# Two more columns at the end of the tokens stage, and sums loaded two joins ahead, in a hybrid decoder step

## The chip, the cores and the metric

The kernel runs on one core of a Trainium2 chip. Times are device microseconds of that core. Three runs of the kernel before took 2443.08, 2441.34 and 2442.59 us; the median is 2442.59.

## What is computed

One inference step of a one-layer hybrid trunk, for a prompt of 2048 tokens and 8 sampled sequences of 4 new tokens (32 tokens), width 1024. Cut to what matters here:

```python
u = rmsnorm(h, norm_mix_g)
proj = u @ w_in                       # q, k, v of A and C | z | xbc | dt
oa = banded_attention(A)              # window 128, with a sink per head
oc = sum over branches of w_b * o_b   # C: (128,1), (512,4), (2048,16), weighted by their denominators
xbc = silu(causal_dwconv(xbc))        # width 4, 1024 channels
dt = softplus(dt_raw + dt_bias); y = ssd_chunked(x, dt, A, B, C) + d_skip * x
ob = rms_normalize(y * silu(z)) * ssm_norm_g
h = h + [oa | ob | oc] @ w_out
h = h + square(relu(rmsnorm(h) @ w_up)) @ w_down
```

## The kernel before, in words

Every float32 product is made of three float16 matmuls (high by high, high by low, low by high). The kernel has three stages, each a block of its own with its own semaphores: `tokens`, `settle` (GpSimd clears semaphores) and `core`.

**The tokens stage** (`tokens`, L92) computes the normed input u, stores its halves, and makes the columns of q, k, v and dt by token. It also turns the weights of the 12 "z" columns (z and xbc, 128 channels each) into halves (`z_w`, two places), stores them to `kept_w`, and makes those columns for the 32 sampled tokens. `Z_ORDER` ends with 4 and 5, so at the end `z_w` holds the weights of the first two columns of the channel phase. Four more, those that were handled first, are loaded back into the ring (`load_ahead`, L328 to L332, semaphore `ahead_in`). Its last units are "ahead" 0, a "half", "silu", a "half" and "ahead" 1 (its `plan`, L162). An "ahead" (L789 to L794) is one column of the channel phase for the first 512 tokens: 24 matmuls of 128x512, whose bank is left to the next stage. SP's queue ends with the last stores and waits until all have landed.

**The core stage** (`core`, L828) first has the channel phase: 4 pieces of 512 tokens by 12 columns, each column four "quarters" of 6 matmuls. Weights of a column come through a ring of 5 places (`fetch`, L1319; `RING`, `RING_AHEAD` and `COL_AHEAD` in L820). ScalarE copies a finished column out of its bank (`take_col`, two instructions), VectorE filters it if it is one of the first 8 (`conv`, three instructions and a copy), and after every fourth column ScalarE has a "silu" with a table load before and behind it.

Beside the quarters, a hand-made plan (`plan`, L1063) hangs the other work on positions 48n + 4i + quarter. Attention begins at 4 COL_AHEAD + 1: 16 tiles of the dilation 16 at a spacing of 3 quarters, then the 12 of the first block at 3 or 4. In slot k TensorE gives values of tile k-3, turns p of tile k-2 and makes the scores of tile k-1. VectorE makes the maxima, ScalarE the exponentials and the high halves of p, VectorE the low halves. "dt" has two parts, at columns 4 and 7 of the first piece (L1090); its first needs eight small loads (`dt_in`, 128) and is work of VectorE and ScalarE alone. The sampled tokens' scan begins at position 38. Then follow the scans of chunks 0 to 3, each with parts at 0, 7 and 11 quarters, and four joins: "weigh" t on VectorE combines the stored outputs and denominators of four attention kinds (`js`, one tile of 128 x 4 x 264, loaded by `load_sums`, L1454), and "turn" t transposes the result on TensorE into u, with copies on ScalarE and subtractions on VectorE. The load of join t+1 waits for join t. A spacing of 6 quarters lies between the joins. "ahead" 0 and 1 in this stage split the first raw weights of "out". "out 0" needs all four turns and the scans' mix, loaded by `load_scanned` after turn 2.

Every engine works through its own instructions strictly in the order of the units, and so does SP, which issues all loads and stores. After the channel phase come "out", the norm, "up" and "down" of each of the four blocks; attention, scans and joins of the next block run beside them.

In the trace, L2421 is every dense matmul of the core stage, L793 those of "ahead" in tokens, L2516, L2531 and L2546 values, turned p and scores, L2752 the turns of joins. L2131 is the filter, L2064 the maxima, L1834 the exponentials, L1827 and L2083 the halves of p, L1767 and L1768 the silu with its loads.

```python
            at = 4 * COL_AHEAD + 1
...
                        if n == 0 and i in (4, 7) and quarter == 0:
                            yield "dt", i // 7, 0, 0
```

Of the kernel before, what the change touches and what calls it, by code (L numbers as in the profile page):

```python
# [91 lines left out]
def tokens(nc, io, before):  # L92

    with ExitStack() as ctx:
# [205 lines left out]
        with nc.Block() as block:  # L301
# [404 lines left out]
            def _(pe):  # L706
# [57 lines left out]
                for kind, n, j, q in units:  # L764
# [24 lines left out]
                    elif kind == "ahead":  # L789
                        free(pe, "ahead", j)  # L790
                        for k in range(KT):
                            for i, (part, s) in enumerate(((0, 0), (0, 1), (1, 0))):
                                pe.matmul(prod[ahead_bank[j]][:, :], z_w[:, j % 2, k, part, :], u[:, 0, s, k, 0:512], start=k == 0 and i == 0,  # L793
                                          stop=k == KT - 1 and i == 2)  # L794
# [25 lines left out]
RING, RING_AHEAD, COL_AHEAD = 5, 4, 2  # L820
# [7 lines left out]
def core(nc, io, before):  # L828

    with ExitStack() as ctx:  # L830
# [30 lines left out]
        R, RW, AHEAD, SP_H = RING, 2, 2, 4  # L861
        NH = KT + SP_H
# [34 lines left out]
        v_lo = a.sb("v_lo", [P, RV, 4, HD + 1], F16)  # L897
        p = a.sb("p", [P, 4, 2 * P])
# [16 lines left out]
        with ExitStack() as early:  # L915
# [60 lines left out]
        js = a.sb("js", [P, 4, OROW])  # L976
        jt = a.sb("jt", [P, 2, 256])
# [7 lines left out]
        js_in, j_step, j_exp, j_ready, j_turned, jh_ready, jl_ready, j_out = (  # L985
            a.sem(s) for s in ("js_in", "j_step", "j_exp", "j_ready", "j_turned", "jh_ready", "jl_ready", "j_out"))
# [76 lines left out]
        def plan():  # L1063
# [17 lines left out]
            for unit in joins(0):  # L1081
                beside[at].append(unit)
                at += 6 if unit[0] == "weigh" else 0
# [197 lines left out]

        def raw_src(q):
# [8 lines left out]
        def loads(q):  # L1291

            return sum(1 for j in range(q % R, q + 1, R) if not raw(j) and j >= RING_AHEAD)
# [22 lines left out]
        with nc.Block() as block:  # L1316
            @block.sync
            def _(sp):
                def fetch(q):  # L1319
# [11 lines left out]
                    else:  # L1331
                        sp.dma_start(ring[:, q % R, :, :, :].rearrange("p k i c -> p (k i c)"), kept_w[home(q), :, :]).then_inc(ring_in[q % R], 16)

                def keep(q):
                    if raw(q):
                        sp.wait_ge(lo_split, raw_no[q] + 1)
                        sp.dma_start(kept_w[home(q), :, :], ring[:, q % R, :, :, :].rearrange("p k i c -> p (k i c)")).then_inc(kept[q % R], 16)
# [116 lines left out]
                def load_sums(t):  # L1454
# [70 lines left out]
                def finish(unit):  # L1525
# [29 lines left out]
                    elif kind == "weigh" and b % 4 < 3:  # L1555
                        load_sums(b + 1)
# [28 lines left out]
                fetch(RING_AHEAD)  # L1585
# [15 lines left out]
                fetched, next_qkv = RING_AHEAD + 1, 3  # L1601
# [1300 lines left out]
```

## Time and profile before

| what | value |
|---|---|
| time of the runs | 2442.59 us median (2441.34 to 2443.08) |
| profiled execution | span 2443.3 us; the page gives no other time for it, and it lies 0.7 us above the median |
| TensorE busy | 2363.2 us (97%), 17246 matmuls |
| VectorE, ScalarE, GpSimd busy | 1216.1 (50%), 817.0 (33%), 272.7 us (11%) |
| DMA | 419.64 MB, mean 172 GB/s |
| granted clock, mean | 0.989 |

### The profile page before, as it was taken

To read this page: it belongs to the slowest core of one execution; us is meant where nothing else is said; L and a number is where in the kernel's file an instruction comes from. 1 tells how busy PE (TensorE), PEld (TensorE's weight loads), DVE (VectorE), ACT (ScalarE), POOL (GpSimd) and SP (SyncE) were. 2 spreads that over 40 slices of the span, in tenths; PEclk is the share of its full clock that TensorE was granted. 3 is DMA by queue.
4 is the path that set the end of the run, shared out by engine and by line. 5 is a ranking of instruction groups with operands and counts; after the bars stand their busy time and mean duration, and the time that the engine had idled before them with its cause. 6 is when DMAs were issued, how large, how long until landed. Compare 5 with 4: busy or idle time off the path is not lost. (4 is left out here: it accounts for less than half of the span.)

```text
span 2443.3 us, 42522 instructions
## 1 busy us (share of the span) xinstructions
PE 2363.2 (97%) x17246; PEld 1374.2 (56%) x17246; DVE 1216.1 (50%) x2785; ACT 817.0 (33%) x1467; POOL 272.7 (11%) x301
## 2 busy tenths in 40 slices
PE   9899889999889999999999999999999999999999
PEld 5456445555435555444555554445555456888887
DVE  5557465656647667742655563145566522322222
ACT  5544244554445444331423222023323111210210
POOL 0111223111011211001120100001111001000000
PEclk9999999999999999999999999999999999999999
DMA  7646496785477876885575565534645553222222
GB/s 254 240 162 229 167 233 168 209 234 172 146 236 180 222 213 214 268 266 164 135 171 154 163 184 159 174 119 129 166 157 170 177 160 122 88 96 96 96 96 85
DMA packets 396561, 419.64 MB, mean 172 GB/s; under 512 B 130319, under 2 KB 325391, under 8 KB 396112
## 3 DMA queue, kind: packets, MB, share of 16 engines
q1 hardware_dynamic: 396368, 416.94, 56.8%
q8 instruction: 137, 2.24, 0.4%
q14 instruction: 56, 0.46, 0.1%
HBM read 280.01 MB, written 118.96 MB: 163 GB/s over the span
## 5 line engine op out<-in xcount | busy, mean ns | idle before, releaser
L2421 PE MATMUL core_dense<-core_u,tok_ring 128*128 128x512 f16 (+2 forms) x4800 | 862.3, 340 | 7.8 <-DVE core_u L2004 7.5
L2421 PEld LDWEIGHTS core_dense<-core_u,tok_ring 128*128 128x128 f16 x4800 | 465.7, 98 | 375.6 <-DVE core_u L2004 11.4
L2421 PE MATMUL core_dense<-core_r_hi,tok_ring 128*128 128x512 f16 (+2 forms) x2560 | 649.9, 339 | 1.2 <-DVE core_r_lo L2023 1.2
L2421 PE MATMUL core_dense<-core_r_lo,tok_ring 128*128 128x512 f16 (+2 forms) x1280 | 434.1, 339 | 0.0
L2421 PEld LDWEIGHTS core_dense<-core_r_hi,tok_ring 128*128 128x128 f16 x2560 | 250.4, 98 | 195.8 <-DVE core_r_lo L2023 1.9
L2421 PE MATMUL core_dense<-tok_u,tok_ring 128*128 128x512 f16 x1104 | 259.9, 393 | 15.1 <-PEq L811 11.0
L2020 DVE TENSOR_TENSOR core_r<-core_r 128x512 f32<-128x512 f32 (+2 forms) x160 | 96.7, 605 | 293.7 <-ACT core_r L1804 293.3
L1804 ACT ACTIVATE core_r<-core_dense 128x512 f32<-128x512 f32 (+2 forms) x160 | 82.4, 515 | 478.9 <-PE core_dense L2421 478.7
L732 PE MATMUL tok_prod<-tok_w_hi,tok_u 128*128 128x512 f16 (+1 forms) x768 | 197.2, 346 | 4.1 <-DVE tok_u L601 4.1
L2421 PEld LDWEIGHTS core_dense<-tok_u,tok_ring 128*128 128x128 f16 x1104 | 107.9, 101 | 147.5 <-issue 27.6
L2421 PEld LDWEIGHTS core_dense<-core_r_lo,tok_ring 128*128 128x128 f16 x1280 | 125.2, 98 | 93.3 <-issue 0.7
L2032 DVE SCALAR_TENSOR_TENSOR core_h<-core_dense,core_h 128x512 f32<-128x512 f32 (+1 forms) x96 | 58.3, 607 | 210.4 <-PE core_dense L2421 210.3
L1834 ACT ACTIVATE core_p<-core_p,core_neg 128x256 f32<-128x256 f32 (+1 forms) x256 | 99.7, 460 | 183.3 <-DVE core_neg L2071 183.3
L732 PE MATMUL tok_prod<-tok_w_lo,tok_u 128*128 128x512 f16 (+1 forms) x384 | 132.9, 346 | 0.0
L1984 DVE SCALAR_TENSOR_TENSOR tok_ring<-core_staged,tok_ring 128x1024 f16<-128x1024 f32 x72 | 89.2, 1239 | 70.9 <-ACT tok_ring L1737 69.4
L1678 POOL TENSOR_TENSOR core_v_hi<-core_v_raw,core_ones 128x256 f16<-128x256 f32 (+1 forms) x82 | 61.2, 747 | 489.9 <-DMA core_v_raw<-out_tok 337.1
L732 PEld LDWEIGHTS tok_prod<-tok_w_hi,tok_u 128*128 128x128 f16 x768 | 73.4, 98 | 69.1 <-DVE tok_u L601 6.7
L2131 DVE SCALAR_TENSOR_TENSOR core_col<-core_conv_raw,core_cw,core_col 128x512 f32<-128x512 f32 x96 | 76.9, 801 | 63.5 <-ACT core_conv_raw L1758 61.2
L2023 DVE TENSOR_TENSOR core_r_lo<-core_r,core_r_hi 128x512 f16<-128x512 f32 (+2 forms) x160 | 96.3, 602 | 17.0 <-DVE core_r L2020 0.5
L2032 DVE SCALAR_TENSOR_TENSOR core_h_more<-core_dense,core_h_more 128x512 f32<-128x512 f32 (+1 forms) x64 | 36.2, 565 | 130.2 <-PE core_dense L2421 130.2
L1714 POOL TENSOR_TENSOR core_ssum<-core_ssum,core_r 128x512 f32<-128x512 f32 (+1 forms) x24 | 30.8, 1284 | 573.2 <-ACT core_r L1783 573.2
L2064 DVE CUSTOM_DVE_ANT_0 core_p<-core_spare,core_bias 128x256 f32<-128x256 f32 (+1 forms) x256 | 81.5, 374 | 23.4 <-PE core_spare L2546 18.0
(317 smaller groups left out, 2590.3 us busy)
## 6 DMA issues: line engine op xcount, KB each, us to landing
tok_ring<-scratch_kept_w SPq DMA_DIRECT2D x262, 512.0 KB, 4.5
scratch_kept_w<-tok_ring SPq DMA_DIRECT2D x72, 512.0 KB, 5.5
core_staged<-in_w_up SPq DMA_DIRECT2D x32, 512.0 KB, 4.8
core_staged<-in_w_down SPq DMA_DIRECT2D x32, 512.0 KB, 4.5
out_tok<-tok_tok SPq DMA_DIRECT2D x16, 644.0 KB, 3.0
core_piece<-in_c_kt SPq DMA_DIRECT2D x32, 288.0 KB, 4.0
core_piece<-in_c_v SPq DMA_DIRECT2D x16, 576.0 KB, 4.6
scratch_sums<-core_o SPq DMA_DIRECT2D x64, 132.0 KB, 3.7
```

The costliest lines, as they stand in the source:

```text
L732: last = pe.matmul(bank[0:nt, 0:w], l, r[:, k, c0:c0 + w], start=k == 0 and i == 0, stop=k == KT - 1 and i == 2, skip_group_check=True)
L1678: pool.tensor_tensor(hi, v, ones[:, 0:w].rearrange("p (h d) -> p h d", d=HD), ALU.mult).then_inc(vh_ready, 1)
L1714: pool.tensor_tensor(ssum[:, 0:w], ssum[:, 0:w], r[:, i % 2, 0:w], ALU.add).then_inc(summed, 1)
L1804: act.activation(r[:, n % 2, 0:w], bank_of["up", b, f, q][:, 0:w], ACT.Relu, scale=1.0 / (WS * HS)).then_inc(r_ready, 1)
L1834: last = act.activation(p[:, hh, cols], p[:, hh, cols], ACT.Exp, bias=neg[:, hh:hh + 1])
L1984: dve.scalar_tensor_tensor(ring[:, q % R, :, 1, :], w_raw[n % RW], WS, ring[:, q % R, :, 0, :], ALU.mult, ALU.subtract).then_inc(lo_split, 1)
L2020: dve.tensor_tensor(r2[:, n % 2, 0:w], r[:, n % 2, 0:w], r[:, n % 2, 0:w], ALU.mult).then_inc(r2_ready, 1)
L2023: dve.tensor_tensor(r_lo[:, f % HF, off:off + w], r2[:, n % 2, 0:w], r_hi[:, f % HF, off:off + w], ALU.subtract).then_inc(rl_ready, 1)
L2032: dve.scalar_tensor_tensor(here, bank_of["down", b, i, q][:, 0:w], HS * HS / WS, here, ALU.mult, ALU.add).then_inc(down_added, 1)
L2064: last = dve.tensor_tensor_reduce(p[:, hh, cols], spare[1 + bank][:, :].rearrange("p (a c) -> p a c", c=2 * P)[:, at, cols], bias[:, BIAS_ ...
L2131: dve.scalar_tensor_tensor(dst, conv_raw[:, i, j:j + 512], cw[:, i, j:j + 1], dst, ALU.mult, ALU.add).then_inc(tap, 1)
L2421: ins = pe.matmul(bank, w[:, k, part, :], s, start=first and j == 0, stop=last and j == 2, skip_group_check=True)
```

## The change

The tokens stage makes four columns ahead instead of two: the first two from `z_w`, the third and fourth from ring places 0 and 1, after a wait for the ring's loads. The core stage's first slot of the ring is then at place 2 (`place_of`), two of its columns are already loaded instead of four, and three loads are issued at the start instead of one. All that hangs on `COL_AHEAD` moves by 8 quarters; the spacing of the first block's joins is 5 quarters instead of 6. A second tile for sums, `js_odd`, lies where p and the beginning of `p_hi` are. The sums of joins b and b+1 are loaded at the second part of a block's first scan, those of join t+2 after "weigh" t.

```diff
 kind == "ahead":
                         free(pe, "ahead", j)
+                        if j >= COL_KEPT:
+                            pe.wait_ge(ahead_in, 16 * RING_AHEAD)
+                        w_ahead = z_w[:, j % 2, :, :, :] if j < COL_KEPT else ring[:, j - COL_KEPT, :, :, :]
...
-RING, RING_AHEAD, COL_AHEAD = 5, 4, 2
+RING, RING_AHEAD, COL_AHEAD, COL_KEPT = 5, 4, 4, 2
...
+        USED = COL_AHEAD - COL_KEPT
+        LOADED = RING_AHEAD - USED
...
+        with ExitStack() as early:
+            js_odd = early.enter_context(nc.sbuf_tensor("core_js_odd", [P, 4, OROW], F32))
         p = a.sb("p", [P, 4, 2 * P])
...
             for unit in joins(0):
                 beside[at].append(unit)
-                at += 6 if unit[0] == "weigh" else 0
+                at += 5 if unit[0] == "weigh" else 0
...
+        def place_of(q):
+            return (q + USED) % R
...
-                    if t:
-                        sp.wait_ge(j_ready, t)
-                    else:
+                    if t >= 2:
+                        sp.wait_ge(j_ready, t - 1)
+                    elif t == 0:
                         sp.wait_ge(ss_out, SS_ALL)
-                    sp.dma_start(js[:, :, :], io["sums"][:, t * P:(t + 1) * P, :].rearrange("k p c -> p k c")).then_inc(js_in, 16)
+                    sp.dma_start(js_of[t % 2][:, :, :], io["sums"][:, t * P:(t + 1) * P, :].rearrange("k p c -> p k c")).then_inc(js_in[t % 2], 16)
...
-                    elif kind == "weigh" and b % 4 < 3:
-                        load_sums(b + 1)
+                    elif kind == "weigh" and b % 4 < 2:
+                        load_sums(b + 2)
...
-                fetch(RING_AHEAD)
+                for q in range(LOADED, R):
+                    fetch(q)
...
-                fetched, next_qkv = RING_AHEAD + 1, 3
+                fetched, next_qkv = R, 3
...
-                    elif kind == "scan" and i == 2 and b % 4 == 3:
-                        load_sums(b - 3)
+                    elif kind == "scan" and i == 1 and b % 4 == 0:
+                        load_sums(b)
+                        load_sums(b + 1)
```

## Rows read from the trace of the kernel before

**Rows 1.** Windows by stage: length, busy us of each engine, clock, DMA share, GB/s.
```profile
309.00:345.00 36.00, 31.71 (x215) 15.03 (x215) 23.38 (x76) 20.64 (x43) 9.22 (x17) 0.91 0.95 228
632.00:684.00 52.00, 42.97 (x184) 19.37 (x183) 31.71 (x98) 20.12 (x32) 0.00 (x0) 0.89 0.58 178
```

**Rows 2.** Timeline of TensorE, 292 to 325 us: start, us, line, operation.
```profile
292.59 5.34 PE L793 MATMUL tok_prod<-tok_u,tok_z_w 128*128 128x512 f16 x24
308.92 8.30 PE L2421 MATMUL core_dense<-tok_u,tok_ring 128*128 128x512 f16 x30 [10.99 <-PEq L811]
...
324.42 0.63 PE L2531 MATMUL core_spare<-core_ident,core_p 128*128 128x128 f32 x4 [2.78 <-ACT core_p L1834]
```

**Rows 3.** The chain of waits in order of time, one column: start, us, what.
```profile
1299.34 5.18 PE core_dense L2421 x24
```

**Rows 4.** Timeline of SP's queue, 305 to 323 us.
```profile
305.20 0.55 SPq L426 DMA_DIRECT2D scratch_xc<-tok_col_s  x1
...
322.66 0.42 SPq L1594 DMA_DIRECT2D core_of_seq<-in_of_seq  x1
```

**Rows 5.** DMA issues of 290 to 345 us: count, KB, us to landing.
```profile
scratch_xc<-tok_col_s SPq DMA_DIRECT2D x1, 128.0 KB, 2.5
...
core_of_seq<-in_of_seq SPq DMA_DIRECT2D x1, 1.0 KB, 1.5
```

**Rows 6.** Timeline of VectorE, 313 to 333 us.
```profile
313.05 2.67 DVE L2131 SCALAR_TENSOR_TENSOR core_col<-core_conv_raw,core_cw,core_col 128x512 f32<-128x512 f32 x3 [11.41 <-ACT core_conv_raw L1758]
...
319.23 2.32 DVE L2131 SCALAR_TENSOR_TENSOR core_col<-core_conv_raw,core_cw,core_col 128x512 f32<-128x512 f32 x3
...
329.56 0.29 DVE L2098 TENSOR_TENSOR core_dt_all<-core_dt_all,core_dt_bias 128x136 f32<-128x136 f32 x1
...
332.94 0.21 DVE L2109 TENSOR_TENSOR core_a_seq<-core_of_seq,core_small 32x64 f32<-32x64 f32 x1
```

**Rows 7.** Timeline of ScalarE, 322 to 342 us.
```profile
322.89 1.28 ACT L1834 ACTIVATE core_p<-core_p,core_neg 128x128 f32<-128x128 f32 x4 [5.66 <-DVE core_neg L2071]
...
337.36 1.28 ACT L1767 ACT_TABLE_LOAD   x1
...
340.58 1.28 ACT L1768 ACT_TABLE_LOAD   x1
```

**Rows 8.** Windows of 2 us, columns as in rows 1.
```profile
310.00:312.00 2.00, 2.00 (x6) 0.73 (x5) 0.00 (x0) 0.82 (x2) 0.24 (x1) 0.50 0.35 71
```

**Rows 9.** Timeline of TensorE, 343 to 351 us.
```profile
343.15 0.19 PE L2516 MATMUL core_spare<-core_v_hi,core_p_hi 128*128 128x65 f16 x1 [1.44 <-issue]
...
350.23 0.19 PE L2516 MATMUL core_spare<-core_v_hi,core_p_hi 128*128 128x65 f16 x1 [1.40 <-DVE core_p_lo L2083]
```

**Rows 10.** Timeline of TensorE, 621 to 685 us.
```profile
621.89 5.35 PE L2421 MATMUL core_dense<-tok_u,tok_ring 128*128 128x512 f16 x24
...
677.27 7.03 PE L2421 MATMUL core_dense<-tok_u,tok_ring 128*128 128x512 f16 x24
684.13 41.60 PE L2421 MATMUL core_dense<-core_u,tok_ring 128*128 128x512 f16 x192
```

**Rows 11.** Waits of VectorE, 640 to 700 us: total, times, longest.
```profile
DVE core_j_m L2243 <- DMA core_js<-scratch_sums: 5.8, 3, 3.5
```

**Rows 12.** Waits of TensorE, 640 to 700 us.
```profile
PE core_spare L2752 <- DVE core_jt L2262: 9.0, 3, 5.1
```

**Rows 13.** Window of L2421 alone: busy of TensorE and its weight loads, clock, DMA, GB/s.
```profile
631.70:684.30 52.60, 41.34 (x169) 17.71 (x170) 0.89 0.57 176
```

**Rows 14.** Timeline of VectorE, 640 to 679 us.
```profile
640.70 0.16 DVE L2243 TENSOR_TENSOR core_j_m<-core_js 128x4 f32<-128x4 f32 x1 [1.67 <-DMA core_js<-scratch_sums]
...
678.16 0.76 DVE L2364 TENSOR_TENSOR core_u<-core_spare,core_u 128x256 f16<-128x256 f32 x2 [0.30 <-ACT core_u L1936]
```

**Rows 15.** DMA issues of 664 to 684 us, columns as in rows 5.
```profile
core_u<-scratch_mix_lo SPq DMA_DIRECT2D x1, 512.0 KB, 7.9
```

More of the change, by code:

```diff
@@ L790, in _ @@
                         free(pe, "ahead", j)
+                        if j >= COL_KEPT:
+                            pe.wait_ge(ahead_in, 16 * RING_AHEAD)
+                        w_ahead = z_w[:, j % 2, :, :, :] if j < COL_KEPT else ring[:, j - COL_KEPT, :, :, :]
                         for k in range(KT):
                             for i, (part, s) in enumerate(((0, 0), (0, 1), (1, 0))):
-                                pe.matmul(prod[ahead_bank[j]][:, :], z_w[:, j % 2, k, part, :], u[:, 0, s, k, 0:512], start=k == 0 and i == 0,
+                                pe.matmul(prod[ahead_bank[j]][:, :], w_ahead[:, k, part, :], u[:, 0, s, k, 0:512], start=k == 0 and i == 0,
                                           stop=k == KT - 1 and i == 2)
@@ L976, in core @@
         js = a.sb("js", [P, 4, OROW])
+        js_of = (js, js_odd)
         jt = a.sb("jt", [P, 2, 256])
@@ L984, in core @@
         j_lo = a.sb("j_lo", [P, 4, P], F16)
-        js_in, j_step, j_exp, j_ready, j_turned, jh_ready, jl_ready, j_out = (
-            a.sem(s) for s in ("js_in", "j_step", "j_exp", "j_ready", "j_turned", "jh_ready", "jl_ready", "j_out"))
+        js_in, j_step, j_exp, j_ready, j_turned, jh_ready, jl_ready, j_out = a.sems("js_in", 2), *(
+            a.sem(s) for s in ("j_step", "j_exp", "j_ready", "j_turned", "jh_ready", "jl_ready", "j_out"))
         J_STEPS = 12
@@ L1291, in loads @@
         def loads(q):
-            return sum(1 for j in range(q % R, q + 1, R) if not raw(j) and j >= RING_AHEAD)
+            return sum(1 for j in range(q % R, q + 1, R) if not raw(j) and j >= LOADED)
         def stores(q):
@@ L1331, in fetch @@
                     else:
-                        sp.dma_start(ring[:, q % R, :, :, :].rearrange("p k i c -> p (k i c)"), kept_w[home(q), :, :]).then_inc(ring_in[q % R], 16)
+                        sp.dma_start(ring[:, place_of(q), :, :, :].rearrange("p k i c -> p (k i c)"), kept_w[home(q), :, :]).then_inc(ring_in[q % R], 16)
                 def keep(q):
@@ L1336, in keep @@
                         sp.wait_ge(lo_split, raw_no[q] + 1)
-                        sp.dma_start(kept_w[home(q), :, :], ring[:, q % R, :, :, :].rearrange("p k i c -> p (k i c)")).then_inc(kept[q % R], 16)
+                        sp.dma_start(kept_w[home(q), :, :], ring[:, place_of(q), :, :, :].rearrange("p k i c -> p (k i c)")).then_inc(kept[q % R], 16)
                 def load_pu(n):
@@ L1736, in split @@
                         act.wait_ge(raw_in[n % RW], 16 * (n // RW + 1))
-                        act.activation(ring[:, q % R, :, 0, :], w_raw[n % RW], ACT.Copy, scale=WS).then_inc(hi_split, 1)
+                        act.activation(ring[:, place_of(q), :, 0, :], w_raw[n % RW], ACT.Copy, scale=WS).then_inc(hi_split, 1)
                 def take_col(n, i):
@@ L1983, in split @@
                         dve.wait_ge(hi_split, n + 1)
-                        dve.scalar_tensor_tensor(ring[:, q % R, :, 1, :], w_raw[n % RW], WS, ring[:, q % R, :, 0, :],
+                        dve.scalar_tensor_tensor(ring[:, place_of(q), :, 1, :], w_raw[n % RW], WS, ring[:, place_of(q), :, 0, :],
                                                  ALU.mult, ALU.subtract).then_inc(lo_split, 1)
@@ L2237, in then @@
                         dve.wait_ge(j_step, J_STEPS * t + count[0])
-                    dve.wait_ge(js_in, 16 * (t + 1))
+                    dve.wait_ge(js_in[t % 2], 16 * (t // 2 + 1))
+                    js = js_of[t % 2]
                     if t:
@@ L2413, in weights @@
                         pe.wait_ge(lo_split, raw_no[q] + 1)
-                    elif q >= RING_AHEAD:
+                    elif q >= LOADED:
                         pe.wait_ge(ring_in[q % R], 16 * loads(q))
-                    return ring[:, q % R, :, :, :]
+                    return ring[:, place_of(q), :, :, :]
                 def thrice(bank, w, k, hi, lo, first, last):
```

## The prediction

> **What bounds it now.** I read the windows by stage first. TensorE is the engine to watch: of the 36 us from 309 to 345 it is busy 31.7, of the 52 us from 632 to 684, where the first block is joined, 43.0 at a mean clock of 0.89 [rows 1]. The change takes no matmul away, so it can gain only TensorE's idle and half-clock time, and it touches two places where there is some: the gap between the stages, and these joins. TensorE's timeline shows the gap [rows 2]. Its list of waits names the joins' turns between 640 and 700 us, and none in later blocks. From "out 0" on only the joins' loads move.
>
> **The gap between the stages.** TensorE's last "ahead" column starts at 292.59 and takes 5.34; the next matmul comes at 308.92, after 10.99 us of idle time [rows 2]. A column of 24 matmuls takes 5.18 us at full clock [rows 3], so two more take 10.4 and end at 308.3. Today the stage's end is set elsewhere: the store of the sampled columns is issued at 305.20 [rows 4] and lands 2.5 us later [rows 5], at 307.7; core starts 1.2 us behind it. If part of that follows TensorE's end instead, core starts between 308.9 (not moved) and 309.5 (all of the 1.2); I take 309.3, 0.4 later. The new wait on "ahead_in" stands in TensorE's queue before column 2. The loads it waits for are issued with "z" 6 to 9, long before, and cost nothing; were they late, the gap would stay empty by as much.
>
> **The start of core pays it back.** Today VectorE filters columns 0 to 2, from 313.05 on, the third from 319.23 to 321.6 [rows 6]; the first scores' maxima follow, then ScalarE's exponentials at 322.89 [rows 7], and TensorE turns p at 324.42 after 2.78 us idle [rows 2]. The change shifts all attention by 8 quarter columns with the columns, but "dt 0" and the first "silu", tied to column 4, stay. So before the first p VectorE now has four filters, dt 0, the filter of column 4 and the maxima. Each start 0.4 later than today: filters from 313.4, two at 3.1 us, two at 2.45, to 324.6. Then dt 0 waits for all eight of its loads. Today the last is issued at 322.66 [rows 4] and lands 1.5 us later [rows 5], 324.2. Two more ring loads of 512 KB stand ahead of it in SP's queue: half a microsecond each to issue (the small one takes 0.42), and they share the engines, at 0.95 here [rows 1]. For that I take 0.9 us, so 326.5; below, nothing (the filters end at 324.6), above, 3 us more. dt 0 takes 3.6 us (329.56 to 333.15 [rows 6]), to 330.1; the filter 2.45, the maxima 1.2, to 333.8. ScalarE too stands behind dt 0: it takes column 4 until 329.4 and then has "silu" with its two table loads, 4.5 us as from 337.36 to 341.86 [rows 7], until 333.9; exponentials 1.3 us. TensorE turns p at **335.2** instead of 324.42: 10.8 later, the 0.4 included, having stood there since about 321, a wait of 14 us for today's 2.78. It then has 8 quarters, 10.4 us, less to do. Gap and start together: **+0.4**, between -1.5 (no load late) and +3.4. The gap is filled, and one of the same size opens behind it.
>
> The Trainium skill ("DMA: Bandwidth & Descriptors", "Queues, rings and completion order") has each DMA engine take its descriptors in ring order, which would put dt's small loads behind the big ones. At that page's 436 GB/s they would be held 2.4 us, an estimate, and p would come 1.5 us later than mine: it speaks against the change.
>
> **Half clock.** From 310 to 312, after the gap, the granted clock is still 0.50, 1.2 GHz [rows 8], and the first 30 matmuls take 8.30 us [rows 2] where 6.5 would do at 2.4. Filling the gap wins these 1.8 us, but they end in the wait for p, and behind that wait a low stretch like this one comes back. Net 0.
>
> **What hides in the new wait.** Today the silu of 337 to 342 us holds up the halves of p: TensorE is idle 1.44 us before 343.15, and 1.40 before 350.23 [rows 9]. dt 0 and this silu are over before 335.2. I take **-2.0** (0 to -2.8).
>
> **Edits that cost nothing.** Columns 2 and 3 lie in spare banks 2 and 1, where the first scores go: TensorE waits there until ScalarE has copied column 3, some 1.1 us, in front of the wait for p, which covers it. "place_of" changes addresses only; columns' weights come 42 times either way (46 slots less 4, 44 less 2). Attention and scans keep their distances to each other and to the filters; each silu meets another part of them, which I leave at 0, within 2 either way. In later blocks load_sums stands at the first chunk's second part, two columns of work after the last attention unit, with SP in step with TensorE, so its stores have landed and nothing queues behind it; js_odd shares p's place, idle by then.
>
> **The joins.** In all they take 56.9 us today, from the end of quarter 163 (621.89 + 5.35 = 627.24) to "out 0" at 684.13 [rows 10]; 46.5 without the 8 quarters that move away. In them, VectorE waits 5.8 us for js in three of four joins [rows 11], TensorE 9.0 for VectorE [rows 12], and its dense matmuls from 631.7 on take 41.3 us for seven columns [rows 13], 5 more than 7 x 5.2. Afterwards VectorE never waits for js, but a join has 5 quarters (6.5 us) instead of 6, and its own 4.8 us (from 640.70 [rows 14] to 645.5) stay. Counting from T, the end of quarter 171: scan 3's sums on TensorE to T+4.7 as today, norm and halves on VectorE to T+8.1, join 0 to T+12.9; TensorE waits 2 us, then turns. Filter, subtraction and join 1 end at T+20.9, 0.8 late. silu 3,1 on ScalarE delays turn 1's copies, so join 2 ends at T+30.1, 2.0 late; join 3 at T+37, in time. Turn 3 now stands behind the last column, not 4 quarters before it. Its copies and subtractions, 1.6 us (677.27 [rows 10] to 678.92 [rows 14]), are uncovered: "out 0" at T+39.4. A load is late next. The scans' mix is loaded after turn 2, and SP's queue now has the raw load for "out 2" ahead of it, which waits for VectorE's split behind join 2. So issue at T+31.9 and two loads; today the second landed 7.9 us after issue [rows 15], 7 to 10 us for the pair: T+40.7 in the middle. Half clock adds 1.0: 41.7 instead of 46.5, **-4.8**; at best -11.6 (no turn waits, full clock), at worst -1 (the quarter less per join eats what the loads give).
>
> **Sum.** +0.4 - 2.0 - 4.8 = -6.4 us on the profiled span of 2443.3, 2436.9. The span is 0.7 above the runs' median of 2442.59; on the median's scale **2436.2 us**.
>
> **Rivals.** (a) The gap is filled and nothing is paid back: -10.4, joins -9.0, half clock -4.5, 2418.7. Against it: VectorE and ScalarE have no way round dt 0. 7%. (The Trainium skill, "TensorE: Matmul & The Clock Gate", "Why this matters for your kernels", has idle gaps between bursts closed to keep the clock up; by that rule alone the change gains.) (b) As forecast, but no turn waits: joins -11.6, 2429. For it: later blocks. 18%. (c) Within 0.2%: joins -1, start 1 worse, silu's gain 1: 2442. For it: VectorE's chain of filter, subtraction and join is longer than 5 quarters. 25%. (d) Slower: dt's loads land far behind the ring loads. It decides from 338 for them, p turned at 346.5; up to there the joins pay. With p at 347.5 it is 2448.5. Against it: they land 1.5 us after issue today [rows 5]. 8%. My own forecast: 42%.
>
> Two tenths of a per cent (4.9 us) is about what a measurement of this kernel can tell from no change. Below 2437.7 lie (a), (b) and most of my own case: 0.60. Within it 0.32, slower 0.08. The range reaches from just beyond (b) to just beyond (c), 2427 to 2443, and leaves out (a), (d) and the bounds' far ends.
>
> **What would show it.** Right: "ahead" without a gap to 308.3; core from 308.9 to 309.5; one wait of TensorE of 12 to 16 us before the first turn of p, with dt 0 ahead of column 4's filter; no wait of VectorE for js; turns' waits of 4 to 5 us in all; 1 to 3 us before "out 0". Wrong: p turned before 331 (then (a)); a gap left before "ahead" 2; new waits over 3 us between 345 and 632; any difference behind "out 0".

## The result and the profile after

| | before | after |
|---|---|---|
| median of the runs, us | 2442.14 (2441.34 to 2443.08) | 2458.53 (2458.08 to 2460.32) |
| ratio, 95% interval | | 1.0065 [1.0053, 1.0077] |
| profiled span, us | 2443.3 | 2456.6 |
| TensorE busy, us | 2363.2 | 2366.6 |

The change makes the kernel slower by 0.65%, 16.4 us on the medians and 13.3 us between the two profiled executions. The forecast was 2436.2 us, with a range of 2427 to 2443: wrong, and on the other side.

The 3.1 us between the two differences lie in the profile of before. In 135 executions of these kernels the time is 1.7 to 3.0 us above the span, 1.9 in the middle; so a span of 2443.3 belongs to an execution of about 2445, an estimate, some 3 us above the median. Two runs with the plan of before (e2 and e11, below) have 217.3 and 217.6 us in the stage from P0 to X0 where this profile has 219.2.

The line numbers of the core stage are 15 higher in the kernel after (14 for VectorE and ScalarE): L2421 is now L2436, turned p L2546, values L2531, the sums of a scan L2682 (before L2667), the joins' turns L2767.

The timeline of TensorE after, 292 to 338 us, answers to [rows 2]:
```profile
292.16 5.34 PE L796 MATMUL tok_prod<-tok_u,tok_z_w 128*128 128x512 f16 x24
297.34 10.52 PE L796 MATMUL tok_prod<-tok_u,tok_ring 128*128 128x512 f16 x48
308.86 6.63 PE L2436 MATMUL core_dense<-tok_u,tok_ring 128*128 128x512 f16 x30 [1.00 <-PEq L814]
316.38 0.51 PE L2561 MATMUL core_spare<-core_qk_t 64*128 64x128 f16 x12 [0.89 <-ACT core_conv_raw L1772]
...
336.07 1.09 PE L2546 MATMUL core_spare<-core_ident,core_p 128*128 128x128 f32 x4 [15.19 <-ACT core_p L1848]
```
The gap is filled, as meant: two more columns in 10.52 us, 1.00 us of idle time, the core stage's first matmul still at 308.9, and its first 30 in 6.63 us for 8.30. And a wait of 15.19 us stands before the first turn of p. So far all is as forecast.

To see where the time went I cut both traces at six events that lie at the same place of the work: the core stage's first matmul, the first turn of p (P0), the 17th turn (P16), the first matmul of chunk 0's scan (X0), the sums of chunk 3's scan (G3) and "out 0". These are the windows of after, with the columns of [rows 1]:
```profile
308.90:336.10 27.20, 11.12 (x61) 4.90 (x61) 16.93 (x38) 14.05 (x22) 6.05 (x14) 0.80 0.85 212
336.10:476.50 140.40, 129.99 (x1019) 71.67 (x1020) 77.84 (x292) 61.63 (x142) 34.96 (x45) 0.91 0.73 199
476.50:563.70 87.20, 83.34 (x769) 46.58 (x768) 51.93 (x183) 50.33 (x95) 10.12 (x16) 1.00 0.73 201
563.70:660.70 97.00, 79.62 (x474) 43.42 (x472) 56.41 (x119) 40.26 (x53) 15.73 (x12) 0.94 0.55 170
660.70:696.70 36.00, 32.27 (x144) 15.56 (x145) 27.50 (x91) 16.75 (x29) 0.00 (x0) 0.92 0.52 157
```
and the same windows of before:
```profile
308.90:324.40 15.50, 12.73 (x60) 5.26 (x61) 9.46 (x21) 6.49 (x12) 6.22 (x14) 0.89 0.81 160
324.40:457.10 132.70, 124.25 (x1019) 69.02 (x1020) 81.01 (x300) 66.29 (x148) 34.55 (x43) 0.95 0.80 216
457.10:543.60 86.50, 83.02 (x770) 46.54 (x769) 52.37 (x183) 50.09 (x96) 11.39 (x18) 1.00 0.77 208
543.60:629.90 86.30, 78.28 (x473) 42.73 (x471) 56.24 (x119) 35.77 (x50) 15.61 (x12) 0.98 0.57 179
629.90:684.10 54.20, 45.16 (x192) 21.34 (x193) 32.63 (x99) 22.20 (x34) 0.00 (x0) 0.88 0.56 172
```
The counts of matmuls show that the cuts are fair: the middle three windows hold the same work, and the last 48 matmuls less, the 8 quarters (10.4 us) that went ahead. Start +11.7, P0 to X0 +8.4, scans +10.7, joins -18.2, all behind "out 0" +0.7: +13.3 us. The joins without the quarters gained 7.8 us. Most of the loss is between P0 and G3. There the change adds nothing but the early loads of the sums; for the rest it shifts attention, scans and joins against what is tied to a column.

The list of waits of TensorE from 563 to 661 us, where the scans are, says on whom (before: 4.1 us in 2, longest 2.7, for the first kind, 2.7 for the second, none of the third):
```profile
PE core_dense L2436 <- ACT core_col L1772: 6.7, 1, 6.7
PE core_spare L2682 <- ACT core_m L1902: 4.8, 1, 4.8
PE core_dense L2436 <- ACT core_conv_raw L1772: 4.6, 1, 4.6
```
All three are for ScalarE, and a silu lengthens each, by three different ways. ScalarE's timeline ahead of the wait for core_conv_raw, which ended at 625.42:
```profile
609.75 1.28 ACT L1781 ACT_TABLE_LOAD   x1
611.04 1.91 ACT L1781 ACTIVATE core_col<-core_col 128x2048 f32<-128x2048 f32 x1
612.97 1.28 ACT L1782 ACT_TABLE_LOAD   x1
614.26 0.38 ACT L1892 ACTIVATE core_b_tok<-core_spare 128x256 f32<-128x256 f32 x1
614.54 1.05 ACT L1894 ACTIVATE core_grown<-core_dec 128x1024 f32<-128x1024 f32 x1
619.45 1.06 ACT L1896 ACTIVATE core_dec<-core_dec 128x1024 f32<-128x1024 f32 x1 [3.85 <-DVE core_dec L2214]
```
A silu of 4.5 us now stands in front of the first work of a scan (b by token), so the scan's later products come late, and the copy of a column, queued behind them on ScalarE, with them. Before, the silu at 599.43 lay behind a scan's products and held up nothing there: ScalarE's next instruction, at 604.38, waited 0.44 us more, for GpSimd.

The next silu, 649.25 to 653.75, holds back the copy of a column, and with it VectorE, whose filter stands in front of the scan's y; y then passes GpSimd and ScalarE before TensorE's sums at 660.68. VectorE's timeline of after:
```profile
655.06 2.33 DVE L2145 SCALAR_TENSOR_TENSOR core_col<-core_conv_raw,core_cw,core_col 128x512 f32<-128x512 f32 x3 [3.27 <-ACT core_conv_raw L1772]
```
The longest wait, 6.72 us before 598.65, goes through SP's queue. The silu of 574.25 ends its work at 577.46; SP waits for it with the store of its result, and the loads of the sums and of chunk 1's rows of decays stand behind that store:
```profile
577.49 0.36 SPq L1361 DMA_DIRECT2D scratch_xc<-core_col  x1
...
578.57 0.89 SPq L1474 DMA_DIRECT2D core_js<-scratch_sums  x1
...
580.80 0.66 SPq L1457 DMA_DIRECT2D core_dec<-scratch_decay  x1
```
and ScalarE has to wait for the rows:
```profile
588.42 1.06 ACT L1894 ACTIVATE core_grown<-core_dec 128x1024 f32<-128x1024 f32 x1 [3.89 <-DMA core_dec<-scratch_decay]
```
The rows' load is issued 17.1 us behind X0; before it was 13.5 (557.13), ahead of the silu's store at 577.73.

### The profile page after: what moved, and what is told of

It reads as the page before. It is cut to its first block and busy times, and to the rows that moved or that the text cites. A ratio compares the mean times of both kernels' runs of the same rounds, so it can differ in the third digit from the quotient of the medians.

```text
span 2456.6 us, 42525 instructions
## 1 busy us (share of the span) xinstructions
PE 2366.6 (96%) x17246; PEld 1376.5 (56%) x17246; DVE 1215.7 (49%) x2785; ACT 817.3 (33%) x1467; POOL 272.7 (11%) x301
## 5 line engine op out<-in xcount | busy, mean ns | idle before, releaser
L2436 PE MATMUL core_dense<-core_u,tok_ring 128*128 128x512 f16 (+2 forms) x4800 | 862.3, 340 | 9.6 <-DVE core_u L2018 7.5
L2436 PEld LDWEIGHTS core_dense<-core_u,tok_ring 128*128 128x128 f16 x4800 | 465.6, 98 | 377.4 <-DVE core_u L2018 11.4
L2436 PE MATMUL core_dense<-core_r_hi,tok_ring 128*128 128x512 f16 (+2 forms) x2560 | 650.0, 339 | 1.2 <-DVE core_r_lo L2037 1.2
L2436 PE MATMUL core_dense<-core_r_lo,tok_ring 128*128 128x512 f16 (+2 forms) x1280 | 434.1, 339 | 0.0
L2436 PEld LDWEIGHTS core_dense<-core_r_hi,tok_ring 128*128 128x128 f16 x2560 | 250.4, 98 | 195.8 <-DVE core_r_lo L2037 1.9
L2436 PE MATMUL core_dense<-tok_u,tok_ring 128*128 128x512 f16 x1056 | 250.1, 395 | 12.4 <-ACT core_col L1772 6.7
L2436 PEld LDWEIGHTS core_dense<-tok_u,tok_ring 128*128 128x128 f16 x1056 | 104.1, 101 | 141.9 <-issue 20.9
L2436 PEld LDWEIGHTS core_dense<-core_r_lo,tok_ring 128*128 128x128 f16 x1280 | 125.2, 98 | 93.3 <-issue 0.7
L2046 DVE SCALAR_TENSOR_TENSOR core_h_more<-core_dense,core_h_more 128x512 f32<-128x512 f32 (+1 forms) x64 | 36.1, 565 | 130.2 <-PE core_dense L2436 130.2
L2078 DVE CUSTOM_DVE_ANT_0 core_p<-core_spare,core_bias 128x256 f32<-128x256 f32 (+1 forms) x256 | 81.4, 373 | 25.6 <-PE core_spare L2561 19.6
```

The costliest lines, as they stand in the source:

```text
L2046: dve.scalar_tensor_tensor(here, bank_of["down", b, i, q][:, 0:w], HS * HS / WS, here, ALU.mult, ALU.add).then_inc(down_added, 1)
L2078: last = dve.tensor_tensor_reduce(p[:, hh, cols], spare[1 + bank][:, :].rearrange("p (a c) -> p a c", c=2 * P)[:, at, cols], bias[:, BIAS_ ...
L2436: ins = pe.matmul(bank, w[:, k, part, :], s, start=first and j == 0, stop=last and j == 2, skip_group_check=True)
```

## The experiments

My theory: units that the plan ties to a column (the silus, "dt", the sampled tokens' scan at 38 + 3k) stayed while attention and scans moved by 8 quarters, and where they now meet, an engine that works in order holds up TensorE. Rivals: the early loads of the sums stand in SP's queue in front of a scan's rows; four columns ahead cost something of their own. The unchanged kernel ran beside each group. Stages are from one profile each; "start" is to P0.

| run | start | P0 to X0 | scans | joins | ratio to before, 95% interval |
|---|---|---|---|---|---|
| before | 15.5 | 219.2 | 86.3 | 54.2 | |
| after | 27.2 | 227.6 | 97.0 | 36.0 | 1.0065 [1.0053, 1.0077] |
| e1_only_ahead | 27.4 | 227.3 | 96.2 | 41.4 | 1.0091 [1.0076, 1.0106] |
| e2_only_sums | 15.5 | 217.3 | 86.1 | 46.9 | 0.9982 [0.9973, 0.9991] |
| e3_scan_moved_too | 27.6 | 223.1 | 98.1 | 36.0 | 1.0060 [1.0045, 1.0075] |
| e4_sums_behind_rows | 26.1 | 232.5 | 96.2 | 36.1 | 1.0078 [1.0061, 1.0094] |
| e5_plan_only | 25.6 | 225.8 | 94.3 | 41.2 | 1.0069 [1.0054, 1.0084] |
| e7_whole_plan | 20.9 | 219.5 | 87.3 | 41.8 | 1.0011 [1.0001, 1.0020] |
| e8_silus_only | 26.3 | 227.7 | 87.3 | 40.3 | 1.0040 [1.0026, 1.0054] |
| e9_dt_only | 20.9 | 227.4 | 97.0 | 36.0 | 1.0039 [1.0024, 1.0054] |
| e10_plan_and_joins | 21.2 | 222.3 | 85.5 | 38.9 | 0.9994 [0.9985, 1.0002] |
| e11_only_sums_again | 15.8 | 217.6 | 86.0 | 47.8 | 0.9985 [0.9976, 0.9994] |
| e12_filters_behind_scores | 13.0 | 227.2 | 87.2 | 38.9 | 0.9983 [0.9974, 0.9991] |

Joins are compared after adding 10.4 us wherever four columns were made ahead or attention was moved (all but before, e2 and e11).

**The two halves of the change.** e1 is after, with the joins' loads of before:
```diff
-                    elif kind == "weigh" and b % 4 < 2:
-                        load_sums(b + 2)
+                    elif kind == "weigh" and b % 4 < 3:
+                        load_sums(b + 1)
...
-                    elif kind == "scan" and i == 1 and b % 4 == 0:
-                        load_sums(b)
-                        load_sums(b + 1)
+                    elif kind == "scan" and i == 2 and b % 4 == 3:
+                        load_sums(b - 3)
```

> The changed kernel with the joins' part undone: one tile of sums, each load one join ahead, issued after the third scan part as before. Four columns are still made ahead and the joins' spacing stays 5. Theory A (work that moved meets work that stayed): TensorE's stretch from the first turn of p to the first one of block 0 stays near 140.4 us (132.7 before). Theory B (the sums' loads stand ahead of chunk 1's rows in SP's queue): the stretch from the first scan to the last scan's sums falls from 97.0 by about 4 us, and ScalarE no longer waits 3.9 us for those rows. The joins lose again: from the last scan's sums to out 0 about 36 + 8 = 44 us. By both the whole is 3 to 6 us slower than the changed kernel.

e2 is after, with the columns and the plan of before:
```diff
-RING, RING_AHEAD, COL_AHEAD, COL_KEPT = 5, 4, 4, 2
+RING, RING_AHEAD, COL_AHEAD, COL_KEPT = 5, 4, 2, 2
...
-at += 5 if unit[0] == "weigh" else 0
+at += 6 if unit[0] == "weigh" else 0
```

> The changed kernel with two columns made ahead, as before, and the joins' spacing back at 6; two tiles of sums and their loads two joins ahead stay. Theory A: everything up to the first scan is as in the kernel before. Theory B: the stretch from the first scan to the last scan's sums is 2 to 4 us over 86.3, through a late load of chunk 1's rows. The joins gain: from 54.2 us to about 43 (no wait of VectorE for sums, no wait of TensorE for a turn). By B the whole is 6 to 9 us faster than the kernel before, without B's cost 11 us.

Measured: e1 2465.65 us, e2 2437.98, before 2442.24. The whole loss comes with the columns (start, P0 to X0 and scans of e1 are those of after), and the sums alone gain: joins 46.9 for 54.2, scans untouched at 86.1. The rival about SP's queue falls for the most part: the loads cost the scans of e2 nothing. Both expectations missed in size: e1 is 7.1 us slower than after where I had 3 to 6, and e2 gains 4.3 us where I had at least 6, since its joins came to 46.9 and not 43; TensorE still waits 4.4 us for two of the turns.

**Sums behind the rows.** The early loads moved behind the rows' load of the next chunk:
```diff
                     elif kind == "scan" and i == 1 and b + 1 < NT:
                         load_rows(b + 1)
+                        if b % 4 == 0:
+                            load_sums(b)
+                            load_sums(b + 1)
```

> The changed kernel with the two loads of sums issued behind the load of chunk 1's rows, not ahead of it. Theory B: ScalarE's wait of 3.9 us for core_dec goes, TensorE's wait of 6.7 us for a bank after it falls to 3 or less, the whole is 3 to 4 us faster. Rival (the silus' new places in the scans make this wait): the rows come early, the wait stays over 5 us, and the time changes by less than 1.5 us.

Measured: ScalarE's wait for the rows falls from 3.9 to 0.9 us and TensorE's behind it from 6.7 to 3.8, nearly as theory B had it. But the scans as a whole only go from 97.0 to 96.2, with 1.6 us less between chunks 1 and 2 (27.6 to 26.0) and 0.8 more behind them. So the order in SP's queue costs about 1 us here. The run as a whole is 4.7 us slower than after, from the stage P0 to X0 (232.5 for 227.6), which comes before the edit, and where TensorE's waits behind P0 are nearly the same (10.9 us in all up to P16, 10.1 in after); its clock is at 0.69 from 372 to 376 and 0.50 from 376 to 380, where after has 1.00. It isn't the profiled execution alone: the four runs took 2460.12 to 2464.76 us, those of after 2458.08 to 2460.32. Why the clock is lower in them isn't shown.

**The sampled scan moved with attention.**
```diff
-beside[38 + 3 * k].append(("sscan", k, 0, 0))
+beside[46 + 3 * k].append(("sscan", k, 0, 0))
```

> The changed kernel with the sampled tokens' scan moved by 8 quarters too (46 + 3k instead of 38 + 3k), so that it stands to attention as before. Theory A: the stretch from the first turn of p to the first one of block 0 falls from 140.4 us to 133 to 135, TensorE's waits for core_o in the sampled scan's sums go from 3.4 us to 0.5, and the whole is 5 to 7 us faster than the changed kernel. Rival (these losses come from the longer start alone, whose delayed work is caught up only later): no change within 2 us.

Measured: 4.5 us less between P0 and X0 (223.1). P0 to P16 takes 135.4 us for 140.4, with TensorE's busy time back at 124.0 us and its clock at 0.95, as before (124.3, 0.95); the 2.7 us that are left to before's 132.7 are idle time. Scans 1.1 more, the whole 2457.62 us, 0.9 less than after where I had expected 5 to 7. Part of the cost, not most of it.

**The plan alone.** The kernel before, with two columns ahead as ever, but attention and what follows 8 quarters later and 5 quarters between joins:
```diff
-            at = 4 * COL_AHEAD + 1
+            at = 4 * COL_AHEAD + 9
-                at += 6 if unit[0] == "weigh" else 0
+                at += 5 if unit[0] == "weigh" else 0
```

> The kernel before with nothing but its plan shifted: attention, scans and joins 8 quarters later in the channel phase (first position 17 instead of 9) and joins 5 quarters apart. Two columns are made ahead, sums have one tile. TensorE has the same columns to do, so the shift by itself costs nothing but its last part; what it costs beyond is the price of meeting silu, dt and the sampled scan, which stay. Theory A (moved work meets work that stayed): from the first turn of p to the first of block 0 it takes 5 us more than the 132.7 of before, from the first scan to the last scan's sums 95 to 97 us instead of 86.3; the whole is 12 to 20 us slower than the kernel before. Rival (the losses come from the four columns made ahead: filters and copies piled up at the start): these stretches stay within 2 us of before, and the whole within 5 us.

Measured: 2460.48 us, slower by 0.69%. This run settles it: there is no third and fourth column ahead, no other ring and no second tile in it, and it shows after's late start (here the 8 quarters themselves fill it), its middle stage within 1.8 us, and in the scans three waits of the same kinds, two of them of the same length:
```profile
PE core_spare L2667 <- ACT core_m L1888: 4.8, 1, 4.8
PE core_dense L2421 <- ACT core_conv_raw L1758: 4.6, 1, 4.6
PE core_dense L2421 <- ACT core_col L1758: 3.8, 1, 3.8
```
Beside e1 (same plan, gap filled) it also shows what the filled gap is worth: P0 comes at 334.8 us here and at 335.9 there. Two columns moved into the gap only lengthen the wait behind it.

**Silus alone, dt alone, and the whole plan.** e8 puts each silu two columns later, e9 the dt units (to columns 6 and 8), e7 both (dt at 6 and 9) and the sampled scan.
```diff
-if quarter == 3 and i % 4 == 0 and (n or i):
+if quarter == 3 and i % 4 == 2 and (n or i > 2):
...
-if n == 0 and i in (4, 7) and quarter == 0:
+if n == 0 and i in (6, 8) and quarter == 0:
```

> The changed kernel with only the silus moved by two columns. Theory A puts the loss in the scans on the silus' new places: from the first scan to the last scan's sums 86 to 89 us instead of 97.0; the first turn of p comes 4 us sooner, since silu 0 no longer stands before the exponentials; the whole 10 to 14 us faster. Rival (sums ahead of the rows, or low clock): the scans' stretch stays over 94 us, the whole within 5 us.

> The changed kernel with dt's two parts at columns 6 and 8 instead of 4 and 7. If dt and the wait for its loads are what lies in the start's chain, the first turn of p comes 21 to 23 us after the start of core instead of 27.2; if the four filters alone set it, over 25. The rest as in the changed kernel (the whole 3 to 6 us faster) unless dt's later place meets attention.

> The changed kernel with all the rest of the plan moved by 8 quarters as well: the sampled scan at 46 + 3k, dt at columns 6 and 9, each silu behind the third column of the next four instead of the first. So all work stands to all other as before, and to the columns. Theory A: first turn of p 21 us after the start of core (27.2 in the changed kernel, 15.5 before: two more filters stay ahead of it), then 133, 87, 86 to 87 and, for the joins, 36 to 38 us; the whole 20 to 25 us faster than the changed kernel, 5 to 12 faster than the kernel before. Rival (pile-up of filters at the start, sums ahead of the rows): the scans' stretch stays over 92 us and the whole is over the kernel before.

Measured: e8 brings the scans from 97.0 to 87.3, e9 the start from 27.2 to 20.9; the other's stage stays nearly where it was (start 26.3 in e8, scans 97.0 in e9). In e8 the rows' load is issued 13.5 us behind X0 again, with the sums' loads still ahead of it, and ScalarE doesn't wait for it. TensorE's timeline in e8 has the three waits of the scans at before's size (2.7, 1.4 and 2.7) or near it:
```profile
594.18 4.16 PE L2436 MATMUL core_dense<-tok_u,tok_ring 128*128 128x512 f16 x12 [2.72 <-ACT core_col L1772]
618.59 2.10 PE L2436 MATMUL core_dense<-tok_u,tok_ring 128*128 128x512 f16 x6 [2.10 <-ACT core_conv_raw L1772]
650.46 1.16 PE L2682 MATMUL core_spare<-core_m,core_ones 128*128 128x128 f32 x8 [1.44 <-ACT core_m L1902]
```
Both kernels as a whole are 4.5 us faster than after. For e9 that is what I expected, for e8 I had 10 to 14: its start came 0.9 us sooner and not 4, since ScalarE then waited for VectorE's maxima until 333.93, its joins are 4.3 us longer, and so is, by 5.2 us, all behind "out 0".

With all three moved (e7) the middle stage is back too, at 219.5 (2 us above e2 and e11), and the kernel at 2445.91 us: of 0.65% lost, 0.11% is left. I had expected 5 to 12 us less than before, so in the whole the rival is right. Its joins are 5.8 us longer than after's, because the last piece's silus now fall among them: on ScalarE the one of 670.33 stands in front of turn 3's copies, which end at 676.93. TensorE's timeline of e7:
```profile
650.12 1.12 PE L2767 MATMUL core_spare<-core_ident,core_jt 128*128 128x128 f32 x4 [6.22 <-DVE core_jt L2277]
...
678.03 22.34 PE L2436 MATMUL core_dense<-core_u,tok_ring 128*128 128x512 f16 x91 [3.70 <-issue]
```
The stretch behind "out 0" took 5.0 us more in e7's profile than before, and 5.9 in e8's. Of that, 2.5 us in e7 and 1.7 in e8 directly follow the wait of 3.70 us that both have there: the first 24 matmuls of "out 0" took 7.7 and 6.9 us for 5.2 before, at a clock of 0.74 and 0.83 in the first 10 us for 1.00. The rest stays open.

**The silus out of the joins' way.** e10 is e7 with the last piece's first silu behind "weigh" 0 and its second at quarter 179, its place in after; e11 repeats e2 beside it. The edit doesn't quite do what the expectation says of it: on ScalarE the first silu (646.42) stands in front of turn 0's copies and the second (658.22) in front of turn 1's, not behind the joins' copies.
```diff
-                        if quarter == 3 and i % 4 == 2 and (n or i > 2):
+                        if quarter == 3 and i % 4 == 2 and (n or i > 2) and not (n == 3 and i > 2):
...
+                        if (n, i, quarter) == (3, 8, 3):
+                            yield "silu", 3, 1, 0
...
                         yield from beside.pop(48 * n + 4 * i + quarter, [])
+                        if (n, i, quarter) == (3, 6, 3):
+                            yield "silu", 3, 0, 0
```

> The changed kernel with every unit that stood at a fixed place of the plan (the sampled scan, the two dt units, the silus) moved with the rest, as in the whole-plan run, but with the last piece's silus put behind scan 3's weighing and behind the joins' copies. My theory (what was lost is all in units that stayed behind while attention and scans moved, the joins' gain is real and independent): first turn of p 20.9 us after the core stage's start, from there to the sampled scan's first matmul 219 to 220, scans about 87, last scan's sums to out 0 36 to 38, span near 2433 and 0.3 to 0.5% faster than before. Rival (two columns more in front of the core stage cost something of their own that no placement gives back): scans or the stage before them stay 5 us or more above these, and the whole is no faster than before.

> The kernel before with only the joins' part of the change, a second time, on the same chip as the two beside it, since its first interval against before was a fifth of a per cent wide about a gain of the same size. My theory: 2434 to 2438 us, faster by 0.2 to 0.35%, last scan's sums to out 0 near 47 where before has 54. Rival (its gain was the spread of runs): within 0.1% of before though the stage is as short.

Measured: e10 2440.79, e11 2438.72, before 2442.84. e10's start, scans (85.5) and joins (38.9) came near what was expected; the whole did not: a span of 2439.5 us where near 2433 was expected. Its turns wait longer than after's, 6.0 us for 2.0:
```profile
PE core_spare L2771 <- DVE core_jt L2281: 6.0, 3, 3.2
```
and its core stage began 1.6 us later than after's. The middle stage took 222.3 us where e7, with the same plan there, took 219.5: the spread between executions, as far as the two profiles tell. e2 and e11, 21 runs of one kernel in two groups, both lie below before, by 0.18% and 0.15%. The rival of e10 is not refuted: with everything moved in step, the two columns in the gap gain nothing over e11, which has neither them nor the shift. e10's median is 2.1 us above e11's, and their intervals overlap.

**VectorE's filters behind the scores.** The wait of 8.9 us that is left before P0 in e10 is VectorE's: four columns' filters stand in front of the first maxima. e12 is e10 with those of columns 2 and up done behind attention units:
```diff
+elif kind == "col" and k == 3 and i < KT and b == 0 and i >= 2:
+    waiting.append(i)
...
 elif kind == "att":
     attention(b, i, k)
+    for _ in range(2 if b == 0 and k else 0):
+        if waiting:
+            conv(0, waiting.pop(0))
```

> The run with the whole plan and the joins, and in addition VectorE's filters of the first piece's columns 2 and up done behind the attention units, up to two in each, all by column 8. My theory (what TensorE waits for at the core stage's start is VectorE's chain, in which the filters of columns made ahead stand in front of the maxima): first turn of p 13.5 to 15 us after the stage's start in place of 20.9, some waits of 1 to 2 us behind it, the whole 4 to 6 us faster than the run without it, near 2428. Rival (the filters come due in the next attention units, whose VectorE work is as tight): the first turn comes earlier but the stage up to the sampled scan is longer by as much, and the whole is the same.

Measured: 2438.41 us, 2.4 us faster than e10 where I had 4 to 6. P0 comes 13.0 us after the start, 8.2 earlier, but X0 only 3.3 earlier (240.2 us from the start for 243.5; e7 has 240.4). TensorE's timeline in e12 has the rest of it:
```profile
321.78 0.63 PE L2559 MATMUL core_spare<-core_ident,core_p 128*128 128x128 f32 x4 [0.90 <-ACT core_p L1852]
...
338.13 0.21 PE L2544 MATMUL core_spare<-core_v_hi,core_p_hi 128*128 128x65 f16 x1 [4.88 <-DVE core_p_lo L2101]
```
The wait went from the maxima to the low halves of p, one engine, one chain. Mostly the rival's case. The intervals of e12 and e10 overlap, though 8 of e12's 11 runs lie below the fastest of e10's.

## Why the prediction was wrong

**The gap: right.** "Ahead" without a gap to 307.9, the wait on "ahead_in" nowhere to be seen, the core stage at 308.9 as before. The +0.4 that I had taken is there, though: the store of the sampled columns was issued at 304.74, 0.46 us sooner than in before's profile, and the core stage began no sooner.

**The start of core: right.** Forecast: P0 at 335.2 behind a wait of 14 us; measured 336.07 and 15.19. VectorE's timeline after answers to [rows 6]:
```profile
321.72 2.32 DVE L2145 SCALAR_TENSOR_TENSOR core_col<-core_conv_raw,core_cw,core_col 128x512 f32<-128x512 f32 x3
...
326.90 0.30 DVE L2112 TENSOR_TENSOR core_dt_all<-core_dt_all,core_dt_bias 128x136 f32<-128x136 f32 x1 [2.66 <-DMA core_of_seq<-in_of_seq]
...
330.29 0.21 DVE L2123 TENSOR_TENSOR core_a_seq<-core_of_seq,core_small 32x64 f32<-32x64 f32 x1
330.54 2.33 DVE L2145 SCALAR_TENSOR_TENSOR core_col<-core_conv_raw,core_cw,core_col 128x512 f32<-128x512 f32 x3
...
333.99 0.17 DVE L2085 TENSOR_SCALAR core_neg<-core_o 128x4 f32<-128x4 f32 x1
```
Filters, dt 0, column 4's filter, maxima, in this order; dt 0 began at 326.90 for a forecast of 326.5. SP's queue shows why it was late:
```profile
314.66 1.73 SPq L1344 DMA_DIRECT2D tok_ring<-scratch_kept_w  x3
...
325.30 0.42 SPq L1607 DMA_DIRECT2D core_of_seq<-in_of_seq  x1
```
The last of dt's loads was issued at 325.30 instead of 322.66 and landed 1.6 us later, for 1.5 before [rows 5]: the time was lost in issuing, not behind the ring's data. I had 1.0 us for issuing two ring loads more, and SP took 1.2 (1.73 us for three, 0.50 for one before); the other 1.5 us are in the transposing load right behind them, 2.95 us to issue for 1.45, which I didn't foresee; why it took longer isn't shown. It took the place of the 0.9 us that I had for shared engines. The estimate from the Trainium skill's rule ("DMA: Bandwidth & Descriptors", "Queues, rings and completion order"), 1.5 us more for descriptors that stand behind the ring loads, is not seen here. Gap and start cost 11.7 - 10.4 = +1.3, forecast +0.4.

**"What hides in the new wait", -2.0: not seen in the sum.** The silu of the first piece is over before P0, and its two waits [rows 9] are gone. Up to P16 TensorE's waits before values are 1.6 us shorter in all, 6.1 for 7.7. But those before the sampled scan's own matmuls are 3.5 longer, 4.0 for 0.5, and TensorE's idle time is 10.4 us for 8.5.

**"Edits that cost nothing": the step that failed.** I wrote that attention and scans keep their distances to each other, that each silu meets another part of them, "which I leave at 0, within 2 either way", and did not weigh the sampled scan's fixed place at all. Both terms are large. The silus cost the scans about 9.7 us (97.0 to 87.3 in e8), as their 4.5 us on ScalarE now stand in front of a scan's first product and before its sums instead of behind them, and the store of one in front of the rows' load in SP's queue. Between P0 and X0 the cost is 8.4 us: 4.5 come back with the sampled scan (e3), all but 0.3 with the three kinds of unit together (e7; 3.1 in e10, with the same plan there). Neither the silus alone (e8, 227.7) nor dt alone (e9, 227.4) give any of it back, so how the rest divides stays open. In the profile most of it is no wait: of the 7.7 us between P0 and P16, 5.7 are busy time for the same 1019 matmuls, at a mean clock of 0.91 for 0.95, and they are gone with the sampled scan moved (e3, 124.0). But e5, with the sampled scan in its old place, has 125.6 us too, so its place alone doesn't decide it. Together +19.1 us where I had 0; with this term the forecast of 2436.9 for the profiled span would have been 2456.0, and 2456.6 was measured, with the misses of the other steps (start +0.9, the new wait +2.0, the joins from G3 on -3.0, +0.7 behind "out 0") nearly cancelling, which is luck. The trace of before had what the step needed: the positions of the silus in the plan, and ScalarE's timeline of one scan, on which I should have moved the silu by 8 quarters, as I did for dt 0 at the start.

**"Half clock", net 0.** At the gap 1.7 us were won (30 matmuls in 6.63 us for 8.30). Behind the new wait a low stretch came back: four turns of p took 1.09 us for 0.63, the 18 dense matmuls behind them 6.21 for 5.75. The further low stretches in the attention stage, above, were not foreseen.

**The joins: right.** From G3 on they gained 7.8 us (36.0 for 54.2 - 10.4). But I had counted from T, the end of quarter 171, with the scan's sums as today: that is 655.86 here, and "out 0" came 40.9 us later for a forecast of 41.7, so -5.6 for -4.8. The other 2.2 us are the longer wait before those sums (4.82 for 2.67), which my -4.8 didn't hold and which is on the scans' account here. VectorE waits for no js any more. TensorE's timeline, all its waits between G3 and "out 0":
```profile
660.68 2.08 PE L2682 MATMUL core_spare<-core_m,core_ones 128*128 128x128 f32 x8 [4.82 <-ACT core_m L1902]
671.50 0.66 PE L2767 MATMUL core_spare<-core_ident,core_jt 128*128 128x128 f32 x4 [0.36 <-DVE core_jt L2277]
679.28 0.66 PE L2767 MATMUL core_spare<-core_ident,core_jt 128*128 128x128 f32 x4 [0.64 <-DVE core_jt L2277]
687.40 0.66 PE L2767 MATMUL core_spare<-core_ident,core_jt 128*128 128x128 f32 x4 [1.00 <-DVE core_jt L2277]
696.72 3.61 PE L2436 MATMUL core_dense<-core_u,tok_ring 128*128 128x512 f16 x16 [1.74 <-issue]
```
The turns wait 2.0 us where I had 4 to 5: TensorE waited 1.00 us for join 2, which I had 2.0 late behind silu 3,1, and 0.36 for join 0, for which I had 2. Before "out 0" there are 1.74, in the 1 to 3 foreseen.

**The rivals.** None is what happened. (d) came out on the right side for another reason, dt's loads, which were 0.4 us late; (a) is refuted by P0 itself and by e5 beside e1: the filled gap is paid back in full. The list of what would show me wrong had it: "new waits over 3 us between 345 and 632", and there are two, at 598.65 (6.72) and 625.42 (4.64).

## What to carry to other kernels

When a written-out order is shifted, list every unit that does not shift with it, and for each engine that works in order lay the unshifted unit on the timeline at its new place; "it meets another part of the work" is a price to be read, here 10 us from silus of 4.5. The queue that issues loads and stores is one of these engines. Idle time of the busiest engine between two stages is worth filling only if that engine was what the next stage's first result waited for: otherwise the wait moves behind the boundary. Where a change has two parts, time them alone; here the small one, two tiles for the sums, gains 0.15 to 0.18%, and no placement of the large one that was tried does clearly better.

## What the runs showed of the hardware

The granted clock fell to 0.50 in a stretch in which TensorE has no idle time in the trace. Windows of after, 368 to 392 us, columns as in [rows 1]:
```profile
368.00:372.00 4.00, 2.79 (x35) 1.60 (x33) 1.63 (x7) 2.97 (x9) 0.00 (x0) 1.00 0.96 279
372.00:376.00 4.00, 3.41 (x28) 2.63 (x28) 3.10 (x15) 1.92 (x6) 0.37 (x1) 1.00 1.36 282
...
380.00:384.00 4.00, 4.00 (x106) 3.74 (x106) 1.78 (x12) 1.72 (x6) 0.00 (x0) 0.90 0.49 110
384.00:388.00 4.00, 4.00 (x57) 3.35 (x56) 0.72 (x4) 0.00 (x0) 0.00 (x0) 0.50 0.00 0
388.00:392.00 4.00, 4.00 (x16) 1.56 (x14) 0.00 (x0) 0.60 (x1) 4.00 (x5) 0.75 0.01 4
```
TensorE had some idle time from 368 to 376, then was busy throughout; from 383.10 on the clock is lower (twenty matmuls of 128x4 in 1.19 us for 0.75). What ran there were the sampled scan's matmuls of 128x4; before shows the same fall at the same work (0.50 from 388 to 392, busy 4.00 of 4.00). TensorE's timeline of after has one shape at both levels:
```profile
381.84 0.75 PE L2619 MATMUL core_spare<-core_grown,core_staged 128*64 128x4 f32 x20
...
385.21 1.23 PE L2619 MATMUL core_spare<-core_grown,core_staged 128*64 128x4 f32 x20
```
What follows pays too: 18 dense matmuls at 387.02 took 5.53 us where 4.06 do at full clock. How much of this a stage gets differs between executions: the same plan of the middle stage took 219.5 and 222.3 us (e7, e10), and 227.6 and 232.5 (after, e4); the plan of before took 217.3, 217.6 and 219.2 (e2, e11, before). Differences of some 3 to 5 us between single profiles of this kernel are therefore read for their waits, not for their sum.
